# Another order of the SBUF allocations in a mixer block and two transformer layers

## The reference

```python
h = rms_norm(x, norm_w)
proj = h @ w_in                      # 1024 x 9224
qkv = silu(causal_depthwise_conv(dn_qkv, conv_w))
o_dn = gated_delta_rule_chunked(dq, dk, dv, g, beta)
...
x = x + (sigmoid(g_dn) * y_dn + sigmoid(g_swa) * y_swa) @ w_out
```

```python
x = x + 0.5 * swiglu(rms_norm_2(x, ffn1_norm[l]), ffn1_w_in[l], ffn1_w_out[l])
h = rms_norm_2(x, mix_norm[l])
z = h @ w_mix_in[l]                  # three attentions: latent, windowed, 2-D neighbourhood
...
x = x + o @ w_mix_out[l]
x = x + mem_xattn(rms_norm_2(x, mem_norm_x[l]), mem, ...)
x = x + 0.5 * swiglu(rms_norm_2(x, ffn2_norm[l]), ffn2_w_in[l], ffn2_w_out[l])
x = rms_norm_2(x, block_norm[l])
```

## Time and profile before

| | |
|---|---|
| median of 3 runs | 3345.42 us (3344.86 to 3345.45) |
| the profiled execution | 3345.42 us |
| its span, first to last instruction | 3343.6 us |
| TensorE busy | 3023.5 us, 90% |
| VectorE, ScalarE, GpSimd busy | 1466.3, 1086.4, 251.8 us |
| mean granted TensorE clock | 0.948 of full speed |
| DMA | 237.92 MB, 71 GB/s on the mean |
| chain that ended last | 4483 pieces |

### The profile page before, as it was taken

How to read it: one execution, slowest core, us unless ns; L and a number is a source line. 1 busy time by engine, 2 the same in 40 slices (tenths; PEclk the granted TensorE clock), 3 DMA queues, 4 the chain that set the end, 5 groups by cost and what they waited for, 6 DMA issues and landing times. The chain is left out here.

```text
span 3343.6 us, 37789 instructions
## 1 busy us (share of the span) xinstructions
PE 3023.5 (90%) x13472; PEld 2368.0 (71%) x13472; DVE 1466.3 (44%) x2022; ACT 1086.4 (32%) x1766; POOL 251.8 (8%) x184
## 2 busy tenths in 40 slices
PE   8778998999899998898799999699998989799997
PEld 5567676677688785476668878488775667668875
DVE  5643255643444324545344432444334444344432
ACT  4411233333222213545242221222223545332221
POOL 0000000000200022000220002200021000120001
PEclk9989899999899999999989999799999999899998
DMA  3100221123222222110122222222231010122221
GB/s 118 44 20 7 85 71 37 44 63 119 76 94 94 98 87 93 34 38 20 63 64 99 94 94 69 73 98 94 99 103 55 30 51 32 38 89 100 94 95 68
DMA packets 69070, 237.92 MB, mean 71 GB/s; under 512 B 10352, under 2 KB 14448, under 8 KB 68208
## 3 DMA queue, kind: packets, MB, share of 16 engines
q1 hardware_dynamic: 66960, 227.87, 20.6%
q10 hardware_dynamic: 2016, 8.84, 0.7%
HBM read 234.58 MB, written 2.10 MB: 71 GB/s over the span
## 5 line engine op out<-in xcount | busy, mean ns | idle before, releaser
L368 PE MATMUL bank<-L_h_hi,L_w_hi 128*128 128x512 f32 x1808 | 725.9, 401 | 76.9 <-DVE L_h_lo L469 39.0
L369 PE MATMUL bank<-L_h_lo,L_w_hi 128*128 128x512 f32 x1808 | 713.9, 395 | 0.0
L370 PE MATMUL bank<-L_h_hi,L_weight_ring_low 128*128 128x512 f32 x1808 | 713.5, 395 | 0.0
L356 ACT CAST L_w_hi<-L_weight_ring 128x1024 fp32r<-128x1024 f32 (+2 forms) x292 | 325.7, 1117 | 996.1 <-PE bank L370 986.1
L362 DVE TENSOR_TENSOR L_weight_ring_low<-L_weight_ring,L_w_hi 128x1024 fp32r<-128x1024 f32 (+2 forms) x292 | 400.5, 1373 | 395.1 <-ACT L_w_hi L356 394.8
L368 PEld LDWEIGHTS bank<-L_h_hi,L_w_hi 128*128 128x128 f32 x1808 | 346.1, 191 | 165.0 <-issue 73.2
L369 PEld LDWEIGHTS bank<-L_h_lo,L_w_hi 128*128 128x128 f32 x1808 | 346.4, 192 | 74.9 <-issue 3.8
L370 PEld LDWEIGHTS bank<-L_h_hi,L_weight_ring_low 128*128 128x128 f32 x1808 | 345.5, 191 | 73.5
L368 PE MATMUL bank<-L_act_hi,L_w_hi 128*128 128x512 f32 x704 | 277.4, 394 | 21.5 <-DVE L_act_lo L539 21.5
L369 PE MATMUL bank<-L_act_lo,L_w_hi 128*128 128x512 f32 x704 | 276.7, 393 | 0.0
L370 PE MATMUL bank<-L_act_hi,L_weight_ring_low 128*128 128x512 f32 x704 | 276.2, 392 | 0.0
(11 more groups left out here) (283 smaller groups left out, 3852.4 us busy)
## 6 DMA issues: line engine op xcount, KB each, us to landing
L_weight_ring<-ffn_in SPq DMA_DIRECT2D x176, 512.0 KB, 3.3
L_weight_ring<-ffn_out SPq DMA_DIRECT2D x64, 704.0 KB, 4.0
B_weight_ring<-w_sqk SPq DMA_DIRECT2D x24, 512.0 KB, 3.3
B_weight_ring<-w_dn SPq DMA_DIRECT2D x16, 512.0 KB, 3.3
B_weight_ring<-w_gate SPq DMA_DIRECT2D x16, 512.0 KB, 3.2
L_weight_ring<-w_sna_qk SPq DMA_DIRECT2D x16, 512.0 KB, 3.3
L_weight_ring<-w_mix_out SPq DMA_DIRECT2D x16, 512.0 KB, 3.3
B_weight_ring<-w_sv SPq DMA_DIRECT2D x12, 512.0 KB, 3.3
```

What stands on the lines that cost most here:

```text
L356: e.copy(hv.high(at)[:, 0:width], sh.ring[:, at % RING, 0:width]).then_inc(hv.w_hi_done, 1)
L368: e.matmul(out, a_hi, b_hi, start=start, stop=False)
L369: e.matmul(out, a_hi, b_lo, start=False, stop=False)
L370: return e.matmul(out, a_lo, b_hi, start=False, stop=stop)
```

## The change

The change moves allocations, in `layer_program` and in `block1_program`, and nothing else. In the layer, `gains` and the scaled q gains are allocated before `Halves`, ahead of the feed-forward tensors; the five small tensors of `Attn` are allocated right behind scores, probs and probsT, and the group sums behind `na_bias`. In block 1, `consts1`, `gains1`, `conv`, the q gains and the gate numbers are allocated before the arena, and `w_hi` of `Halves1` behind it.

```diff
@@ layer_program
         sh = Shared(nc, sc, banks, xT, ones, own_h=False)
+        gains = sc.sb("gains", N_GAINS)
+        qg = sc.sb("scaled_q_gains", 4)
+
         with ExitStack() as ffn_memory:
             hv = Halves(sc, ffn_memory, sh.ring_lo)
         jb = Jobs(sc, hv.tmp, hv.up)
         hv.full = [hv.tmp[:, 0, :], hv.tmp[:, 1, :], jb.g[:, 0, :], jb.g[:, 1, :]]
-        big = [sc.sb(n, 2, T) for n in ("scores", "probs", "probsT")]
+        at_ = Attn(sc, T, [4, 5], [2, 3], [6, 7], [sc.sb(n, 2, T) for n in ("scores", "probs", "probsT")],
+                   4 * TT)
         qk = sc.sb("qk", 8, T)
         memT = sc.sb("memT", KT, NMEM)
         na_bias = sc.sb("na_bias", NH, 7 * P)
+        gsum = sc.sb("group_sums", 12)
         cs2 = sc.sb("rope_cos_sin", T)
         swa_bias = sc.sb("swa_bias", 4, 3 * P)
         flat = sc.sb("area", 18 * T)
-        gains = sc.sb("gains", N_GAINS)
-        qg = sc.sb("scaled_q_gains", 4)
-        gsum = sc.sb("group_sums", 12)
-        at_ = Attn(sc, T, [4, 5], [2, 3], [6, 7], big, 4 * TT)
@@ block1_program
         zs = sc.sb("silu_z", 2 * NH, T)
+        consts1 = sc.sb("consts1", N_CONSTS1)
+        gains = sc.sb("gains1", N_GAINS1)
         val_first = sc.sb("first_values", TT, NH * HD)
-        hv = Halves1(sc, sh.ring_lo)
+        conv = sc.sb("conv", 12, CONV)
+        qg = sc.sb("scaled_q_gains", NG)
+        ab = sc.sb("gate_numbers", 10, TT * NH)
...
         with ExitStack() as whole:
             arena = sc.sb("arena", N_ARENA, ctx=whole)
         arena_r = sc.sb("arena_rounded", N_ARENA, dtype=F32R)
-        consts1 = sc.sb("consts1", N_CONSTS1)
-        gains = sc.sb("gains1", N_GAINS1)
-        conv = sc.sb("conv", 12, CONV)
-        qg = sc.sb("scaled_q_gains", NG)
-        ab = sc.sb("gate_numbers", 10, TT * NH)
...
         swa_hi, swa_lo = rounded(16, NH, T), rounded(20, NH, T)
+        hv = Halves1(sc, sh.ring_lo)
         for i in range(2):
             hv.elsewhere[V_FIRST + 2 + i] = rounded(44 + 2 * i, KT * P)
```

## The result

The changed kernel takes 3380.06 us in the median of 4 runs (3377.03 to 3381.43), the kernel before 3345.14 (4 runs, 3343.51 to 3345.45). The ratio is 1.011, with a 95% interval of 1.0098 to 1.0122: 35 us slower, beyond the range of 3341 to 3350. The profiled execution took 3384.5 us, its span is 39.1 us longer.

What follows compares the result with a forecast made beforehand. The prediction took TensorE's instruction stream to bound the kernel. Moved layer tensors, block 1's shifted arena and w_hi, and transfers each added 0: 3345.4 + 0 + 0 + 0 = 3345.4 us, range 3341 to 3350 us.

Steps and rivals of the forecast that it cites:

- What bounds the kernel: Whole kernel: TensorE's instruction stream sets the time, busy 3023.5 us, 90% of the span; one matmul costs about 0.227 us.
- Part 1: Layer: tensors moved by 320 to 704 bytes cost 0 ns per instruction, since matmul medians agree across operand pairs.
- Rival 2: L469, low half of h: faster if congruent addresses of residual and h_hi slowed it; at most 24.8 us won, chance 0.03.
- the first part: Opening of the prediction, on what bounds the kernel: feed-forward matmul starts put one at about 0.227 us.
- Part 2: Block 1: arena and w_hi starting 32 bytes past a multiple of 64 cost 0 ns per instruction.
- Bound of both parts: Address costs in layer and block 1: 1 ns at each of 4483 chain pieces, 4.5 us either way, taken as 0.
- Part 3: DMA transfers into moved tensors (arena table, layer tables, gains): landings stay hidden even at twice the time, 0 us.
- Rival 1: Block 1's 3620 matmuls: rows straddling one more 64-byte SBUF line cost 7.1 ns each, 25.7 us, 3371 us; chance 0.04.
- Rival 3: Layer's gains: the new place looks like an earlier load but no issue moves, 3345.4 us; chance 0.90 together with the forecast.

Runs made afterwards that it cites:

- the layer by 64: Kernel before with 64 unused bytes ahead of Halves in the layer, moving w_hi, h and act while the weight ring stays: 3373.89 us, ratio 1.0091.
- block 1's half: Kernel before with only block 1's allocations moved as in the change, the layer untouched: 3350.04 us, ratio 1.0019.
- 32, 64, 128, 192 and 224: Kernel before with that many unused bytes behind w_hi in the layer, moving only the moving rows, unsplit and up: 3383.27, 3362.87, 3386.36, 3391.02 and 3388.35 us.

## Why the prediction was wrong

- **What bounds the kernel.** Right, and the reason for the size: TensorE's three lines set the time all along, so 4.4 ns on a pitch of 226.7 reach the end undiminished in the layers. In block 1, by their starts in the two traces, the 2112 rounded matmuls take 8.9 us more, but the block grew by 5.6 only. Waits did not hide the rest: TensorE idles 875 - 780.12 = 94.9 us before and 880.6 - 785.53 = 95.1 after. Its other matmuls take 3.5 us less there, and why was not isolated.
- **Part 1, the layer's moved tensors.** This step failed. It costed 320 to 704 bytes at 0 ns, and they cost 33.5 us. Its evidence was that five of six pairs of tensors all over the partition have one median. But those tensors lie in step with each other, all of them: the rows varied the place and kept the one quantity that matters. They could not have shown the effect (in every one of these pairs the two operands are a multiple of 256 bytes apart). Rival 2 had even written down that nearly all large tensors begin at the same place modulo 1 KB, and took this for a possible harm. The second fault is the quantity. The median duration of L368 stayed at 389 in the layer by 64, which lost 30 us; the pitch, which I had worked out in the first part, is what the stream pays.
- **Part 2, block 1's arena and w_hi at 32 past 64.** Failed in the same way: 0 ns by rows of other instructions, VectorE's taps and eight-column weight loads; measured 5.6 us in the profile, and 6.2 us between the medians of block 1's half and of before on one chip. That VectorE pays nothing for such starts was right: its busy time in block 1 is 411.78 and 411.79 us. It says nothing of TensorE.
- **Bound of both parts.** 1 ns on each of 4483 pieces was a residue of the wrong rows on the wrong count. It should have been that of the pitch of rounded matmuls, and for an unseen distance no row gave an upper end.
- **Part 3, transfers.** Right: landings of 10.0, 7.2 and 1.8 us, none of which TensorE waits for; VectorE does wait for gains, before and after alike. The estimate by the Trainium skill's rule in "DMA: Bandwidth & Descriptors", How a descriptor splits into AXI transactions (one more transaction, which by its table holds for a row of whole multiples of 256 bytes as na_bias has, not for every descriptor), stays unseen: na_bias lands in 10.0 us where 10.1 stood before, and 0.2 us cannot be told from that.
- **Rival 1.** Right in sign, and near in size (3371 us) by luck: it had all of its 25.7 us in block 1, which lost 5.6, and none in the layers, which lost 33.5. Wrong in mechanism, for all large tensors of the layers start at multiples of 64 bytes before and after. Its point against itself, that a TensorE which pays for addresses would not show one median over all pairs, is the fault of Part 1 again. The Trainium skill's rule of 16-byte lines, in "SBUF — State Buffer", Specifications (TRN2), by which nothing would change, does not describe this: every shift tried is a multiple of 32 bytes, and all slow the matmuls down but that by 256 and that of everything together. The measurement decides.
- **Rival 2.** The premise was there with the wrong sign: losing the coincidence costs. L469 stayed at 1522 ns.
- **Rival 3.** Right that no load came earlier.

**Open.** Where the reads of weights and of moving rows meet was not isolated, and no rule that gives the price for a distance came out. Most means are 16 cycles apart for three matmuls, 1632, 1648, 1664, 1680, but 1670 and 1685 do not fit. Nor are those means steps of each group of three: in the layer by 64 the groups repeat about 1644, 1656, 1708 and 1648 cycles, 1664 on the mean, while before every one takes 1632. The order of 32, 64, 128, 192 and 224 is unexplained. Distances that are not multiples of 32, and other shapes than 128x512, were not tried.

## What to carry to other kernels

If an edit moves tensors that TensorE reads in rounded products, work out the distance modulo 256 bytes between the weights and the moving rows before and after, and pad it back to what it was; two unused allocations of 192 and 224 bytes were worth 1% here. Judge TensorE by starts per microsecond in a window without idle time, not by the duration of one line's matmuls. And when many rows agree on "no effect", ask whether they differ in the quantity that the change moves.

## What the runs showed of the hardware

The pitch of a rounded 128x512 matmul with a new weight tile each time depends on where its operands stand to each other: 544 cycles (226.7 ns) with weights and moving rows a multiple of 256 bytes apart, 549 to 562 in the other arrangements tried. Moving all tensors together by 64 bytes is free (ratio 1.0001). The growth is there with all other engines and the DMA engines standing still, too (231.1 ns). Plain float32 products showed no dependence in the one line looked at (429 ns), and VectorE, ScalarE and GpSimd none in their busy times (within 1 us in each stage). The Trainium skill, in "TensorE: Matmul & The Clock Gate", Step-by-step: what each phase is for, says that loading the next tile's weights doesn't take read bandwidth from the running matmul. In step no run here contradicts it; out of step the pitch grows by up to 3%, whether the weights or the moving rows were moved.
